# Layer 0's rows begin with token 0 and its products are split 256 and 272, across the border of two PSUM banks

## The reference

```
h = concat(meta, x)                                   # (528, 1024)
for layer in (0, 1):
    if layer == 0:
        u, q, k, v = split(h @ w_in_ab)               # 4 x 512 columns
        mix = concat(s5(u) with GLU, stick_breaking(q, k, v)) @ w_out_ab
    else:
        q, f, i, g = split(h @ w_in_c)                # 4 x 1024 columns
        mix = hgrn2(q, f, i, g) @ w_out_c
    h   = LN(alpha * h + mix)
    hid = relu(h @ w_up + b_up) ** 2                  # 4096 wide
    h   = LN(alpha * h + hid @ w_down + b_down)
return h[16:]
```

## Time and profile before

| | us |
|---|---|
| median of 3 runs | 1563.24 (1561.13 to 1563.93) |
| span of the profiled execution, first to last instruction | 1573.2 |
| TensorE matmuls busy in it | 1419.7 (90%) |
| TensorE weight loads busy in it | 1227.9 (78%) |
| VectorE, ScalarE, GpSimd busy | 756.5, 543.0, 604.2 |
| mean granted TensorE clock | 0.928 |

### The profile page before, as it was taken

How to read it: one execution, slowest core, us unless ns; L and a number is a source line. 1 busy time by engine, 2 the same in 40 slices (tenths; PEclk the granted TensorE clock), 3 DMA queues, 4 the chain that set the end, 5 groups by cost and what they waited for, 6 DMA issues and landing times.

```text
span 1573.2 us, 20067 instructions
## 1 busy us (share of the span) xinstructions
PE 1419.7 (90%) x8518; PEld 1227.9 (78%) x8518; DVE 756.5 (48%) x1123; ACT 543.0 (35%) x794; POOL 604.2 (38%) x233
## 2 busy tenths in 40 slices
PE   6976539998979999999997999999897999999996
PEld 5976534445969999999996888988665888888874
DVE  7995994444465410243136358566457430144134
ACT  4254315554252221222235334324534222232222
POOL 2425512221354343343454323224464443434450
PEclk9988857777989999999999999999999999999997
DMA  5311000000213232333321212111122233332311
GB/s 161 105 54 54 1 1 1 0 1 27 81 41 95 81 107 81 94 95 82 107 81 54 59 49 81 54 53 55 55 79 75 86 107 84 104 101 87 107 54 54
DMA packets 142041, 108.15 MB, mean 69 GB/s; under 512 B 8096, under 2 KB 139376, under 8 KB 141952
## 3 DMA queue, kind: packets, MB, share of 16 engines
q1 hardware_dynamic: 141552, 106.77, 22.9%
q10 hardware_dynamic: 400, 0.11, 0.0%
HBM read 104.77 MB, written 2.10 MB: 68 GB/s over the span
## 4 chain that ended last, share of the span: by engine, by line
PE 75%; DVE 15%; ACT 5%; issue 2%; POOL 2%; DMA 0%; DVEq 0%; SPq 0%; POOLq 0%; ACTq 0%
PE pb L638 56%; PE pb L863 2%; DVE h L1785 2%; PE pb L696 2%; PE pb L697 2%; PE pb L698 2%; DVE uqk L1597 2%; PE pb L882 2%; PE pb L852 2%; PE pb L706 1%; DVE h L1771 1%; PE pb L961 1%; PE pb L867 1%; POOL sqs L508 1%; DVE h L1756 1%
## 5 line engine op out<-in xcount | busy, mean ns | idle before, releaser
L492 POOL TENSOR_TENSOR wl<-raw,wh 128x2048 fp32r<-128x2048 f32 x97 | 453.5, 4676 | 700.5 <-ACT wh L1057 700.5
L638 PE MATMUL pb<-hh,wh 128*128 128x264 f32 (+1 forms) x1376 | 361.7, 322 | 30.0 <-ACT hh L1271 19.5
L638 PE MATMUL pb<-hh,wl 128*128 128x264 f32 (+1 forms) x1376 | 354.9, 317 | 0.0
L638 PE MATMUL pb<-hl,wh 128*128 128x264 f32 (+1 forms) x1376 | 349.0, 315 | 0.9 <-POOL hl L524 0.9
L638 PEld LDWEIGHTS pb<-hh,wh 128*128 128x128 f32 x1376 | 230.7, 192 | 53.0 <-issue 25.9
L638 PEld LDWEIGHTS pb<-hh,wl 128*128 128x128 f32 x1376 | 230.0, 192 | 15.5
L638 PEld LDWEIGHTS pb<-hl,wh 128*128 128x128 f32 x1376 | 227.3, 191 | 17.7 <-POOL hl L524 1.8
L638 PE MATMUL pb<-hidh,wh 128*128 128x264 f32 (+1 forms) x768 | 205.4, 322 | 3.5 <-POOL wl L492 3.5
L638 PE MATMUL pb<-hidh,wl 128*128 128x264 f32 (+1 forms) x768 | 203.4, 319 | 0.0
L638 PE MATMUL pb<-hidl,wh 128*128 128x264 f32 (+1 forms) x768 | 202.6, 318 | 0.0
L1057 ACT ACTIVATE wh<-raw 128x2048 fp32r<-128x2048 f32 x97 | 184.9, 1906 | 1.5 <-DMA raw<-in_w_in_c 1.5
(11 more groups left out here) (344 smaller groups left out, 1923.0 us busy)
## 6 DMA issues: line engine op xcount, KB each, us to landing
raw<-in_mlp_w_up SPq DMA_DIRECT2D x32, 1024.0 KB, 5.4
raw<-in_mlp_w_down SPq DMA_DIRECT2D x32, 1024.0 KB, 5.5
raw<-in_w_in_c SPq DMA_DIRECT2D x16, 1024.0 KB, 5.4
raw<-in_w_in_ab SPq DMA_DIRECT2D x8, 1024.0 KB, 5.7
raw<-in_w_out_ab SPq DMA_DIRECT2D x4, 1024.0 KB, 4.8
raw<-in_w_out_c SPq DMA_DIRECT2D x4, 1024.0 KB, 4.8
x_tok<-in_x SPq DMA_DIRECT2D x2, 1024.0 KB, 8.2
out_h<-o_tok SPq DMA_DIRECT2D x4, 512.0 KB, 3.1
```

The lines of the kernel that those rows point to most:

```text
L492: pool.tensor_tensor(wl[:, c % RING, :], raw[:, c % RING, :], wh[:, c % RING, :].bitcast(F32), ALU.subtract).then_inc(w_lo, 1)
L638: mm = pe.matmul(pb[:, bank + b, 0:z_ - a], lhs, rhs[:, a:z_], start=first and hi and k == 0, stop=last and k == len(todo) - 1)
```

## The change

Rows of layer 0 begin at token 0 in column 0 of the buffers, without lead; layer 1 keeps its lead (`hh1`, `hl1`, and `hidden_rows` with the lead for the stages in `TOK`). The two products of a pair take tokens 0 to 255 and 256 to 527, so 256 and 272 columns. The first writes columns 256 to 511 of its bank and the second columns 0 to 271 of the next, so that a tile's 528 results are one unbroken run of PSUM columns (`line_of`), and the readers take one run in place of two. The f stages of layer 1 take the new split too, on rows that still begin at column 112.

```diff
+SPLIT = 256
-        hh = sb("hh", [P, KC, LEAD + L], F32R)[:, :, LEAD:]
-        hl = sb("hl", [P, KC, LEAD + L], F32R)[:, :, LEAD:]
+        hh_rows = sb("hh", [P, KC, LEAD + L], F32R)
+        hl_rows = sb("hl", [P, KC, LEAD + L], F32R)
+        hh, hl = hh_rows[:, :, 0:L], hl_rows[:, :, 0:L]
+        hh1, hl1 = hh_rows[:, :, LEAD:], hl_rows[:, :, LEAD:]
...
-        hidh = sb("hidh", [P, 16, LEAD + L], F32R, m2)[:, :, LEAD:]
-        hidl = sb("hidl", [P, 16, LEAD + L], F32R, m2)[:, :, LEAD:]
+        hidh_rows = sb("hidh", [P, 16, LEAD + L], F32R, m2)
+        hidl_rows = sb("hidl", [P, 16, LEAD + L], F32R, m2)
...
-            return [(0, NMETA, L)] if name in TOK else [(0, 0, LH), (1, LH, L)]
+            return [(0, 0, NMETA, L)] if name in TOK else [(0, SPLIT, 0, SPLIT), (1, 0, SPLIT, L)]
...
-            return pb[:, b, :] if name in TOK else pb[:, b:b + 2, 0:LH]
+            return pb[:, b, :] if name in TOK else line_of(b)
+
+        def line_of(b):
+
+            return pb[:, b:b + 2, :].rearrange("p a b -> p (a b)")[:, SPLIT:SPLIT + L]
+
+        def inputs(name):
+
+            return (hh1, hl1) if name[-2:-1] == "1" or name[0] in "fqig" and name != "glu" else (hh, hl)
+
+        def hidden_rows(name):
+
+            lead = LEAD if name in TOK else 0
+            return hidh_rows[:, :, lead:lead + L], hidl_rows[:, :, lead:lead + L]
...
-            return ap[:, NMETA:L] if name in TOK else halves(ap)
+            return ap[:, NMETA:L] if name in TOK else ap
...
-                    for b, a, z_ in spans(name):
-                        mm = pe.matmul(pb[:, bank + b, 0:z_ - a], lhs, rhs[:, a:z_], start=first and hi and k == 0,
+                    for b, at, a, z_ in spans(name):
+                        mm = pe.matmul(pb[:, bank + b, at:at + z_ - a], lhs, rhs[:, a:z_], start=first and hi and k == 0,
                                        stop=last and k == len(todo) - 1)
...
-                    run(f"down{layer}{half}", hidh, hidl, lambda k: (hid_ready, seen + k + 1), cols_=P, kcs=16,
+                    run(f"down{layer}{half}", *hidden_rows(f"down{layer}{half}"), lambda k: (hid_ready, seen + k + 1), cols_=P, kcs=16,
...
-                        act.activation(flat(name, hh[:, m, :]), hm, ACT.Identity, bias=b).then_inc(ln_hi, 1)
+                        act.activation(flat(name, (hh1 if n else hh)[:, m, :]), hm, ACT.Identity, bias=b).then_inc(ln_hi, 1)
```

More of the change, by code:

```diff
@@ L523, in lows_ln @@
                         pool.wait_ge(ln_hi, 8 * n + m + 1)
-                        pool.tensor_tensor(flat(name, hl[:, m, :]), flat(name, h[:, m, :]),
-                                           flat(name, hh[:, m, :].bitcast(F32)), ALU.subtract).then_inc(ready, 1)
+                        xh, xl = (hh1, hl1) if n else (hh, hl)
+                        pool.tensor_tensor(flat(name, xl[:, m, :]), flat(name, h[:, m, :]),
+                                           flat(name, xh[:, m, :].bitcast(F32)), ALU.subtract).then_inc(ready, 1)
             pool.memset(ident[:, :], 0.0).then_inc(consts, 1)
@@ L665, in run_after @@
                 s0, _, t0, _ = STAGES[name]
+                xh, xl = inputs(name)
                 arrived(s0)
@@ L672, in run_after @@
                         for k in range(2):
-                            products(name, k, s0, kc * 256 + k * P, hh[:, kc, :], hl[:, kc, :], kc == 0, False, lo=False)
+                            products(name, k, s0, kc * 256 + k * P, xh[:, kc, :], xl[:, kc, :], kc == 0, False, lo=False)
                     if kc >= 1:
@@ L676, in run_after @@
                         for k in range(2):
-                            mm = products(name, k, s0, (kc - 1) * 256 + k * P, hh[:, kc - 1, :], hl[:, kc - 1, :], False,
+                            mm = products(name, k, s0, (kc - 1) * 256 + k * P, xh[:, kc - 1, :], xl[:, kc - 1, :], False,
                                           kc == KC, hi=False)
@@ L680, in run_after @@
                                 mm.then_inc(tile_done, 1)
-                run(name, hh, hl, first=1)
+                run(name, xh, xl, first=1)
             def run_tok(name, starts, pieces=None):
                 s0, slots, t0, _ = STAGES[name]
+                xh, xl = inputs(name)
                 per = len(starts)
@@ L695, in run_tok @@
                             w = slice(kc * 256, (kc + 1) * 256)
-                            pe.matmul(o, hh[:, kc, a:a + rows], wh[:, c % RING, w], start=kc == 0, stop=False)
-                            pe.matmul(o, hh[:, kc, a:a + rows], wl[:, c % RING, w], start=False, stop=False)
-                            mm = pe.matmul(o, hl[:, kc, a:a + rows], wh[:, c % RING, w], start=False, stop=kc == KC - 1)
+                            pe.matmul(o, xh[:, kc, a:a + rows], wh[:, c % RING, w], start=kc == 0, stop=False)
+                            pe.matmul(o, xh[:, kc, a:a + rows], wl[:, c % RING, w], start=False, stop=False)
+                            mm = pe.matmul(o, xl[:, kc, a:a + rows], wh[:, c % RING, w], start=False, stop=kc == KC - 1)
                         mm.then_inc(tile_done, 1)
@@ L703, in ones @@
             def ones(name, b, w, src, first, last):
-                for k, a, z_ in spans(name):
-                    mm = pe.matmul(pb[:, b + k, 0:z_ - a], w[:, :], src[:, a:z_], start=first, stop=last)
+                for k, at, a, z_ in spans(name):
+                    mm = pe.matmul(pb[:, b + k, at:at + z_ - a], w[:, :], src[:, a:z_], start=first, stop=last)
                 return mm
@@ L736, in mlp @@
                     else:
-                        run(f"up{layer}1", hh, hl)
+                        run(f"up{layer}1", *inputs(f"up{layer}1"))
                     seen = 16 * (2 * layer + half)
-                    run(f"down{layer}{half}", hidh, hidl, lambda k: (hid_ready, seen + k + 1), cols_=P, kcs=16,
+                    run(f"down{layer}{half}", *hidden_rows(f"down{layer}{half}"), lambda k: (hid_ready, seen + k + 1), cols_=P, kcs=16,
                         between=ln_parts(2 * layer + 1, 16) if half else None)
@@ L994, in pair @@
                     keys(a)
-                    run(f"f{p}", hh, hl, between=in_f)
-                run(f"q{p}", hh, hl, between=in_q)
+                    run(f"f{p}", hh1, hl1, between=in_f)
+                run(f"q{p}", hh1, hl1, between=in_q)
                 run_tok(f"i{p}", [(0, NMETA)] + [(NMETA + t * P, P) for t in range(4)], in_i)
@@ L1013, in _ @@
             keys(6)
-            run("g", hh, hl, between=in_g)
+            run("g", hh1, hl1, between=in_g)
             s0 = STAGES["out_c"][0]
@@ L1107, in to_uqk @@
             def to_uqk(t, o, par):
-                return act.activation(halves(uqk[:, t, :]), o, ACT.Copy, scale=64.0 ** -0.5 if t // 4 == 1 else 1.0)
+                return act.activation(uqk[:, t, :], o, ACT.Copy, scale=64.0 ** -0.5 if t // 4 == 1 else 1.0)
             def to_tok(dst, rows=lambda k: P):
@@ L1694, in _ @@
                     dve.wait_ge(tile_done, t0 + m + 1)
-                    TS(halves(tmp[:, (t0 + m) % 2, :]), dense("glu", m), cols_b[:, 48 + m:49 + m], -GATE_MAX,
+                    TS(tmp[:, (t0 + m) % 2, :], dense("glu", m), cols_b[:, 48 + m:49 + m], -GATE_MAX,
                        ALU.add, ALU.max).then_inc(emptied_by["dve"], 1)
@@ L1791, in hidden @@
                 freed = 2 + tmp_before(name)
+                xh, xl = hidden_rows(name)
                 for t in range(16):
@@ L1796, in hidden @@
                     me.step(TT(a, r, r, ALU.mult))
-                    TT(flat(name, hidh[:, t, :]), r, r, ALU.mult).then_inc(tmp_free, 1)
+                    TT(flat(name, xh[:, t, :]), r, r, ALU.mult).then_inc(tmp_free, 1)
                     me.settle()
                     dve.wait_ge(tmp_free, freed + t + 1)
-                    TT(flat(name, hidl[:, t, :]), a, flat(name, hidh[:, t, :].bitcast(F32)), ALU.subtract).then_inc(hid_ready, 1)
+                    TT(flat(name, xl[:, t, :]), a, flat(name, xh[:, t, :].bitcast(F32)), ALU.subtract).then_inc(hid_ready, 1)
             def mlp(layer):
```

2 lines of the change are left out of this document (1 added, 1 removed).

## The result

The changed kernel is slower: the ratio to before is 1.0064 with a 95% interval of 1.0040 to 1.0089, the medians of 14 runs each are 1574.7 and 1563.84 us. 0.64% is 10.0 us (6.3 to 13.9). That lies inside my range of 1555 to 1580 us, but outside the likeliest case's own range of 1562 to 1568, and on the side to which I had given 0.39. The single profiled executions don't show it in their spans: 1573.2 us before, 1573.0 after. Some executions of either kernel are about 10 us longer at a lower mean granted clock, and the profiled one before (0.928, against 0.932 in the one after) is like them, so the two spans can't be set against each other. Layer 0's gap-free stretches at the full clock can.

What follows compares the result with a forecast made beforehand. TensorE's gap-free products were taken as the bound. Terms 0.4 (long, hh) + 1.3 (long, hidh) + 0.5 (v) gave +2.2 us on the median 1563.24, so 1565.4 us (+0.14%), range 1555 to 1580 for 8 in 10.

Steps and rivals of the forecast that it cites:

- likeliest case: Whole kernel: +2.2 us, 1565.4 us, own range 1562 to 1568; together with no change it had chance 0.43.
- my second case: Whole kernel: the outcome slower than the 0.2% that a measurement can tell, 3.1 us; chance 0.39.
- slower rival: Layer 0's pairs: 272 columns take 126.6 ns, a pair 246.6; 14 to 18 us more, centre 1579; in full or part 0.33.
- My own signs: Trace after the change: up00 pairs 0.24 us apart, MLP piece of 2646 products within 316 to 321 us.
- What bounds the kernel: TensorE, busy 90% of the span; in the stages touched, each ns on a product comes out at the end.
- the larger of two: Any product's distance: 120 ns for loading 128 columns, or 0.443 to 0.447 ns times its columns, whichever is larger.
- Short product: First product of a pair, 264 to 256 columns: stays at 120.0 ns because of its load, gaining nothing.
- Long product from hh: 272 columns streamed from hh: 120.3 ns, +0.3 on each of 1488 pairs (f included), +0.4 us.
- Long product from hidh: 272 columns streamed from hidh, rows 64 bytes over a multiple of 512: 121.7 ns, +1.7 x 768 pairs, +1.3 us.
- Stage v: Token rows loaded from hh, moved onto a multiple of 512 bytes: 117.6 to 120.0 ns on 192 products, +0.5 us.
- Border and readers: PSUM readings in one run over a bank border: taken as 0, bounds +2.2 us and -0.7 us.
- faster rival: Layer 0's pairs: aligned rows let the short product go at 113.7 or 117.6 ns, giving 1550 or 1558 us; chance 0.18.

Runs made afterwards that it cites:

- the split alone: The changed kernel with layer 0's rows put back behind their lead of 112 columns; ratio to the kernel before 1.0037 (1.0009 to 1.0065).

## Why the prediction was right or wrong

The time fell into my range, and its sign was my second case; the mechanism that I gave was wrong. The likeliest case had +2.2 us where 10.0 came, and the range reached far enough only because it was stretched for the slower rival, so that part is luck. My own signs said as much: the MLP piece took 323.93 us and not 316 to 321, and the pairs of up00 244 ns and not 240. By its own steps:

- **What bounds the kernel**: right. All of the loss is in gap-free trains of products. An estimate from the windows, with every stage at the pace read in it: 1296 pairs of hh at +4 ns 5.2 us, 384 of down00 at +6.7 2.6 us, 384 of down01 at +3.4 1.3 us, v 0.9: 10.0 us, against 10.0 measured (6.3 to 13.9).
- **The step that failed**: "the larger of two: 120 ns for a load of 128 columns, and 0.443 to 0.447 ns times its columns". There is no such floor. With 128 columns loaded, 256 went at 113.4 ns in the second half of v, in the very trace that I had, and at 117.6 in the that I read; with 16 loaded the 264 didn't get faster (121.3). The even beat of the loads was no pacemaker: the same loads come every 244 ns when the pairs do. In its place stands a cost of about 7 to 13 ns on each product of 256 to 272 columns, which depends on the length and on where the streamed operand stands relative to the loaded one. The prediction had named that itself as what would make it wrong ("if the load is no floor, for then the pair's sum depends on how a product's rows lie in memory").
- **Short product**: 120.0 expected. Alone at relative 0 it is 120.0, in up00's pairs after the change 119.5. The i stage was the right row for it, but for the wrong reason.
- **Long product from hh**: the mis-sized term. I had 120.3, a train of them takes 125.3, and in up00's pairs 124.7 stand behind it; the pair is 244 and not 240.3. Times 1296 pairs that is 5.2 us and not 0.4.
- **Long product from hidh**: I had +1.7 ns for the pair, measured +6.7 in down00 and +3.4 in down01: 3.9 us and not 1.3.
- **f stages**: +0.3 ns expected, nothing measured (240 at 448 after the change, 240 before).
- **Stage v**: 117.6 to 120.0 is right for its first half. The second half went from 113.4 to 120.0, which no term had, so the stage cost 96 x 2.4 + 96 x 6.6 ns = 0.9 us and not 0.5. Its reason, the place of the loaded rows, was the one thing in my own working that spoke of place, and I carried it into no other term.
- **Border and readers**: right, 702 ns, and nothing measurable in the whole.
- **The slower rival** had the long product right (126.6 against 125.3) and the pair of hh too high (246.6 against 244), so 14 to 18 us where 10 came. **The faster rival** had it the wrong way round: rows on a multiple of 512 are a dear place for these products, given weights on one.
- **Against the Trainium skill's rule** (TensorE: Matmul & The Clock Gate, Back-to-back issue gap: columns/2.4 + 2.5 ns, given for an isolated product at the full clock): a pair would be 225.0 before and after. The traces show 240 and 244, and for 512 columns 226.7 to 233.3 where the rule has 215.8. The section names no influence of where operands lie; here that is worth up to 6.7 ns on a pair and 6.6 on a product of 512 columns.

A table of what was seen, by place of the streamed operand relative to the loaded one, in bytes modulo 512 (ns for a pair, or for a single product of 256 or 512 in a train of its kind; 128 columns loaded):

```
relative place   256 + 272       264 + 264                 256             512
0                244 or 246.7    240 (0, 32)               120.0           226.7
64               243.4 or 246.7  244 (64, 96)              113.3 or 117.7  229
128              244.5 or 246.7  -                         -               -
192              240             -                         -               233.3
256              244 or 246.7    -                         -               227
384              246.7           244.5 or 246.7 (384, 416) -               233.3
448              240             240 (448, 480)            113.3 or 117.8  233.3
```

The column of 256 holds stages v and i too, where the weights are streamed and the rows loaded. Lines that are 256 bytes apart agree (0 and 256, 192 and 448; 128 and 384 in their slower pace), so the period may well be 256.

Open: why the good places differ with the length, what picks between two paces at one place (it stayed the same through the whole of down00 after the change, and in the down01 of the split alone it changed at a pause of TensorE), and whether the period is 256 or 512 (320 was not tried). Only multiples of 64 bytes, and 32 past them for the second product of 264, were tried. That load and stream get in each other's way when they read the partition's memory is a guess, argued from the place effect's going away with the small load; no run shows it directly.

## What to carry to other kernels

When a train of products is the bound, a product's cost over its bare columns is worth measuring for each length at each relative place of rows and weights, in one kernel with a lead of its own for each stage; an alignment that helps one length (512 columns at 0) can cost another (256 and 272 at 0). Two kinds of product at the same distance are no proof of a floor: look through the same trace for one product below it (the second half of v was one), and take the suspected cost away (load less) before building on it. When a stage is compared by its pace, read more than one train, since one place had two paces. And a result bank's border cost nothing measurable to read across.

## What was unexpected of the hardware

- Moving only the weights by 448 bytes, with the rows untouched, moved 512-column products from 226.6 to 229.1 ns, and in the changed kernel a pair at 448 from 240 to 244.
- With 16 of 128 columns loaded, products of 264 columns went at 121.3 ns, slower than the 119.9 with 128 loaded, and 256 + 272 took 240 ns at both places tried, where a train of 256 alone takes 113.7 for each product.
- With 128 columns loaded, 256 columns went at 113.4 ns in one half of stage v and at 117.6 in the other, before the change, and at 120.0 in both after it.
- The same stage form at the same relative place (down00 and down01 after the change, relative 64) ran at 246.8 and 243 ns for a pair, and out_ab and up00 (relative 0) at 246.7 and 244.
